# Conditioning products of a two-layer decoder step: six chunk products made three pairs in column halves of TensorE, four chunk buffers, gate spreads between product groups

## The reference

```python
for l in range(DEPTH):
    mod = jax.nn.silu(c) @ w_ada[l] + b_ada[l]          # c: (1 or 8, 1024), w_ada[l]: (1024, 3072)
    shift, scale, gate = jnp.split(mod[:, None, :], 3, axis=-1)
    h = rms_norm(x, g_pre[l]) * (1.0 + scale) + shift
    y, ... = mixer_ab(h, ...) if l == 0 else mixer_c(h, ...)
    x = x + gate * rms_norm(y, g_post[l])
```

## Time and profile before

| what | us |
|---|---|
| median of 3 runs | 2801.58 |
| lowest, highest run | 2794.62, 2807.85 |
| the profiled execution, its own time | 2795.68 |
| its span, first to last instruction | 2793.6 |
| PE busy in it | 2570.5 |
| the conditioning products (line 231), layer 0 | 11.09 to 68.05 |
| the first group of the input product starts | 77.47 |
| the conditioning products, layer 1 | 1005.32 to 1078.36 |

### The profile page before, as it was taken

How to read it: one execution, slowest core, us unless ns; L and a number is a source line. 1 busy time by engine, 2 the same in 40 slices (tenths; PEclk the granted TensorE clock), 3 DMA queues, 4 the chain that set the end, 5 groups by cost and what they waited for, 6 DMA issues and landing times. The chain is left out here.

```text
span 2793.6 us, 53877 instructions
## 1 busy us (share of the span) xinstructions
PE 2570.5 (92%) x20904; PEld 1518.9 (54%) x20968; DVE 1331.8 (48%) x2933; ACT 931.6 (33%) x2672; POOL 773.7 (28%) x849
## 2 busy tenths in 40 slices
PE   7989999999699997997999999985899999999997
PEld 2434444444456642443444444445787888888883
DVE  3230303020478854791653625523566666666535
ACT  2432323133111113442231322234454554545421
POOL 1341101001111111552000000005546465655431
PEclk9899999999899998998999999997999999999977
DMA  8341111122364544653121111115423131313112
GB/s 274 111 147 49 65 64 69 49 72 79 127 211 150 180 137 131 169 153 88 55 74 42 68 58 42 57 49 166 130 66 97 63 100 59 104 55 108 40 39 76
DMA packets 257067, 270.50 MB, mean 97 GB/s; under 512 B 31937, under 2 KB 191057, under 8 KB 256820
## 3 DMA queue, kind: packets, MB, share of 16 engines
q1 hardware_dynamic: 185318, 217.40, 23.9%
q10 hardware_dynamic: 71520, 49.96, 6.5%
HBM read 179.96 MB, written 87.36 MB: 96 GB/s over the span
## 5 line engine op out<-in xcount | busy, mean ns | idle before, releaser
L553 PE MATMUL inc_b<-raw_next,inc_w_hi 128*128 128x512 bf16 (+1 forms) x1522 | 459.0, 383 | 11.7 <-DVE raw_next L470 8.4
L553 PE MATMUL inab_b<-inab_wt,inab_h 128*128 128x512 f16 (+1 forms) x1632 | 360.6, 384 | 13.0 <-POOL inab_wt L506 13.0
L553 PE MATMUL inc_b<-raw_next,inc_w_lo 128*128 128x512 bf16 x734 | 281.0, 383 | 0.0
L553 PEld LDWEIGHTS inab_b<-inab_wt,inab_h 128*128 128x128 bf16 (+3 forms) x1632 | 162.1, 100 | 209.5 <-issue 24.4
L553 PEld LDWEIGHTS inc_b<-raw_next,inc_w_hi 128*128 128x128 f16 x1536 | 151.1, 99 | 190.1 <-DVE raw_next L470 7.6
L462 POOL TENSOR_TENSOR keep<-keep 128x1024 f16<-128x1024 f32 (+1 forms) x26 | 58.3, 2243 | 561.8 <-ACT keep L457 561.8
L553 PE MATMUL inab_b<-inab_h,inab_wc_hi 128*128 128x512 f16 (+4 forms) x712 | 178.9, 346 | 10.6 <-DVE inab_h L470 8.0
L553 PE MATMUL inc_b<-inc_w_hi,raw_next 128*128 128x512 f16 (+2 forms) x784 | 167.1, 311 | 16.9 <-POOL inc_w_lo L506 16.9
L1037 PE MATMUL mixab_y<-keep,mixab_oT_hi 128*128 128x512 f16 (+1 forms) x544 | 163.7, 383 | 5.4 <-DVE mixab_f_y L1063 5.4
L1935 DVE SCALAR_TENSOR_TENSOR inc_acc<-inc_ub,inc_taps,inc_acc 128x512 f32<-128x512 f32 x192 | 152.1, 792 | 6.8
L1842 ACT ACTIVATE inc_ub<-inc_b 128x512 f32<-128x512 f32 x96 | 57.0, 594 | 264.8 <-PE inc_b L553 260.6
(11 more groups left out here) (434 smaller groups left out, 5326.0 us busy)
## 6 DMA issues: line engine op xcount, KB each, us to landing
tmp_qkv<-inc_so SPq DMA_DIRECT2D x96, 256.0 KB, 2.0
mixc_qkv<-tmp_qkv SPq DMA_DIRECT2D x15, 1536.0 KB, 7.7
inc_stage<-in_w_in_c ACTq DMA_DIRECT2D x32, 512.0 KB, 4.5
inab_wt<-in_w_ada SPq DMA_DIRECT2D x6, 2048.0 KB, 9.9
inab_stage<-in_w_in_ab ACTq DMA_DIRECT2D x24, 512.0 KB, 4.1
mixab_cw<-in_w_ada ACTq DMA_DIRECT2D x6, 2048.0 KB, 8.2
keep<-in_x_prompt SPq DMA_DIRECT2D x16, 512.0 KB, 4.7
tmp_v<-inab_vz SPq DMA_DIRECT2D x32, 256.0 KB, 3.8
```

Source lines behind the costliest of these rows:

```text
L553: last = nc.tensor.matmul(dst, lhs(a, k), rhs(b, k), start=(k == 0 and i == 0), stop=(k == KT - 1 and i == len(PASSES) - 1))
```

## The change

It computes the same. Two chunks, 2j and 2j + 1, form a pair: their matmuls alternate k by k, the even chunk's nine rows go to partitions 0 to 8 of one bank, the odd one's to partitions 64 to 72, and so to two column halves of the array. `mod`, `gpre` and `gpost` are kept in the same two row ranges, `load_small` issues six transfers in place of three, and `cond.turn` waits once between its halves.

In layer 0 there are four chunk buffers (the fourth in the room of the low-half channel weights, so POOL's first weight units wait until pair 1 is done), chunk 3 is loaded before tile 2, the tables after chunk 5, and weight unit 0 is loaded after `first_square(2)` and rounded inside the loop. PE's order is turn 0, pair 0, turns 1 and 2, half of pair 1, turn 3, the other half, `cond.turn`, pair 2. The first group waits for h k by k and no longer for the gates; the gates are spread after groups 1 and 3. In layer 1 there are three buffers, the small loads come at the end of the prompt, pairs take the place of the chunks in halves, and DVE's adds come in another order.

```diff
+    def rows(self, n):
+        return slice(n % 2 * HB, n % 2 * HB + C9)
+
+    def part(self, n):
+        return self.mod[self.rows(n), n // 2 * 512:(n // 2 + 1) * 512]
...
+        for e in range(2):
+            bias = self.io["b_ada"][l:l + 1, :].rearrange("o (j e n) -> o j e n", j=3, e=2)[:, :, e, :]
+            eng.dma_start(self.mod[self.rows(e)].rearrange("c (j n) -> c j n", j=3), bias.to_broadcast([C9, 3, 512])).then_inc(self.small_in, 16)
+            for dst, src in ((self.gpre, "g_pre"), (self.gpost, "g_post")):
+                eng.dma_start(dst[self.rows(e)], self.io[src][l:l + 1, e * 512:(e + 1) * 512].to_broadcast([C9, 512])).then_inc(self.small_in, 16)
...
+    def pair(self, pe, j, ks=range(KT)):
+
+        for n in (2 * j, 2 * j + 1):
+            pe.wait_ge(self.w_in[n % self.ring], 16 * (n // self.ring + 1))
...
-        for k in range(KT):
-            last = self.nc.tensor.matmul(self.psM[n][0:C9, :], self.cT[:, k, :], self.w[n % self.ring][:, k, :],
...
+        for k in ks:
+            for n in (2 * j, 2 * j + 1):
+                last = self.nc.tensor.matmul(self.psM[j][self.rows(n), :], self.cT[:, k, :], self.w[n % self.ring][:, k, :],
+                                             start=(k == 0), stop=(k == KT - 1))
+        if KT - 1 in ks:
+            last.then_inc(self.mm, 2)
...
+        for e in range(2):
+            if e:
+                pe.wait_ge(self.even_turned, 1)
+            r = self.rows(e)
+            for n in (e, e + 2):
+                for i in range(4):
+                    k = 4 * n + i
+                    last = self.nc.tensor.transpose(self.psT[:, k * C9:(k + 1) * C9], self.part(n)[:, i * P:(i + 1) * P], self.ident[r, r])
+            last.then_inc(self.modtr if e else self.even_turned, 1)
...
+            before = [i for i in range(j) if self.psG[i] is self.psG[j]]
+            if before:
+                pe.wait_ge(self.gate_ready, before[-1] + 1)
+            sel, n = (self.sel, P) if j < 2 else (self.sel_s, NS)
+            self.nc.tensor.matmul(self.psG[j][0:n, :], sel[self.rows(j), :], self.part(4 + j % 2), start=True, stop=True).then_inc(self.spread, 1)
...
-    cond = Cond(nc, ph, 0, io, modT, ring, w_room[0:C9, 12288:12288 + 3 * D], w_room[0:C9, 15360:15360 + D], r_flat[0:C9, 0:D],
+    ring = [a.rearrange("p (k n) -> p k n", k=KT) for a in (
+        *(w_room[:, i * 4096:(i + 1) * 4096] for i in range(3)),
+        w_chan[1][:].rearrange("p k n -> p (k n)").bitcast(F32)[:, 0:4096])]
...
+    GATES = {1: (0, 1), 3: (2, 3)}
...
+        cond.load(sp, 3)
+        for t in range(2):
+            sp.wait_ge(prep.xnd, t + 1)
+            prep.load(sp, t + 2, t, P)
+        cond.load(sp, 4)
+        cond.load(sp, 5)
...
-        for t in range(TPB):
-            if 3 + t < Cond.CH:
-                cond.load(sp, 3 + t)
-            sp.wait_ge(prep.xnd, t + 1)
-            prep.load(sp, t + 2, t % 2, P)
+        for t in range(2):
+            sp.wait_ge(prep.xnd, t + 3)
+            prep.load(sp, t + 4, t, P)
...
+        sp.wait_ge(ctr, 1)
         sp.wait_ge(cT_ready, 1)
         sp.dma_start(io["cT"], cT[:].rearrange("p k c -> p (k c)")).then_inc(cond.out, 16)
+        sp.sem_inc(u_free, 1)
+        for n in range(4):
+            sp.sem_inc(vz_out[n], 16)
         cond.store(sp)
         sp.wait_ge(cond.out, 48)
-        sp.sem_inc(u_free, 1)
         sp.sem_inc(r_free, 1)
-        for n in range(4):
-            sp.sem_inc(vz_out[n], 16)
...
+        pool.wait_ge(cond.mm, 4)
         for u in (0, 1):
...
+            if t == 0:
+                weights.load(act, 0)
             if t == 1:
-                weights.load(act, 0)
-        weights.hi(act, 0)
+                weights.hi(act, 0)
         weights.hi(act, 1)
         cond.take(act)
+        act.wait_ge(cond.modT_ready, 1)
+        act.sem_inc(evac, RING)
         prep.first_low(act, cond.modT_ready, m_a, m_v, first_hi)
         weights.hi(act, 2)
-        cond.gates(act)
         weights.hi(act, 3)
         act.wait_ge(small_in, 32)
-        act.wait_ge(cond.gate_ready, 4)
-        act.sem_inc(evac, RING)
...
-        dve.wait_ge(cond.small_in, 48)
-        for t in range(TPB):
+        dve.wait_ge(cond.small_in, 96)
+        prep.norm(dve, 0, 0, P)
+        prep.raw_high(dve, 0)
+        prep.norm(dve, 1, 1, P)
+        cond.add(dve, 0)
+        cond.add(dve, 1)
+        prep.raw_high(dve, 1)
+        for t in (2, 3):
             prep.norm(dve, t, t % 2, P)
             prep.raw_high(dve, t)
-            cond.add(dve, t)
+        cond.add(dve, 2)
+        cond.add(dve, 3)
+        prep.first_high(dve, cond.modT_ready, m_v, first_hi, first_lo_p, first_lo_v)
+        for n in (4, 5):
+            cond.add(dve, n)
...
-        for t in range(TPB):
-            cond.chunk(pe, t)
-            prep.turn(pe, t, P)
+        prep.turn(pe, 0, P)
+        cond.pair(pe, 0)
+        prep.turn(pe, 1, P)
+        prep.turn(pe, 2, P)
+        cond.pair(pe, 1, range(KT // 2))
+        prep.turn(pe, 3, P)
+        cond.pair(pe, 1, range(KT // 2, KT))
         cond.turn(pe)
-        for n in (4, 5):
-            cond.chunk(pe, n)
-        cond.spread_gates(pe)
+        cond.pair(pe, 2)
...
+        def first_ready(k):
+
+            pe.wait_ge(first_hi, k + 1)
+            pe.wait_ge(first_lo_v if k % 2 else first_lo_p, k // 2 + 1)
+
+        def groups(b, n, next_tiles, first=False):
+            if not first:
+                pe.wait_ge(prep.h_ready, b + 1)
...
+                if first and g in GATES:
+                    cond.spread_gates(pe, GATES[g])
...
-    ring = [ph.sb(f"cw{i}", [P, KT, 512]) for i in range(2)]
+    ring = [ph.sb(f"cw{i}", [P, KT, 512]) for i in range(3)]
...
+    mod = ph.sb("mod", [P, 3 * 512])
+    gpre, gpost = (a[:].rearrange("p g d -> p (g d)") for a in (S1, U))
...
-        cond.load_small(sp)
...
+        sp.wait_ge(state_ready, nt)
+        cond.load_small(sp)
         store(nt - 1, 1, (nt - 1) // 2, P, 0)
 
-        sp.wait_ge(state_ready, nt)
...
-        for n in range(2):
+        for n in range(3):
             cond.load(act, n)
         with act.Fori(3, nt) as t:
             tile(t)
         fin.square(act, nt - 2, P, 1)
         oT_copy(nt - 1, P)
-        cond.load(act, 2)
...
-        dve.wait_ge(cond.small_in, 48)
-        cond.add(dve, 0)
...
+        dve.wait_ge(cond.small_in, 96)
+        cond.add(dve, 0)
         cond.add(dve, 1)
         by_sequence(0)
         dve.wait_ge(o_done, nt + 1)
         src = lambda h: head(obank, h)[0:NS]
         stats(nt, NS, src)
         norm_gate(nt, 0, NS, src)
+        oT_rest(nt, NS)
+        by_sequence(1)
         cond.add(dve, 2)
-        oT_rest(nt, NS)
         cond.add(dve, 3)
-        by_sequence(1)
...
-                cond.add(dve, 4 + p)
+            if p == 1:
+                cond.add(dve, 4)
+                cond.add(dve, 5)
...
-        cond.chunk(pe, 0)
+        cond.pair(pe, 0, range(KT // 2))
...
-        cond.chunk(pe, 1)
+        cond.pair(pe, 0, range(KT // 2, KT))
...
-        cond.chunk(pe, 2)
+        cond.pair(pe, 1, range(KT // 2))
...
-        cond.chunk(pe, 3)
+        cond.pair(pe, 1, range(KT // 2, KT))
...
-                cond.chunk(pe, 4 + p)
+                cond.pair(pe, 2, range(4 * p, 4 * p + 4))
```

More of the change, by code:

```diff
@@ L546, with product @@
 PASSES = ((0, 0), (0, 1), (1, 0))
-def product(nc, dst, lhs, rhs):
+def product(nc, dst, lhs, rhs, before=lambda k: None):
     for k in range(KT):
+        before(k)
         for i, (a, b) in enumerate(PASSES):
@@ L837, in groups @@
                     weights.hi(act, unit_at[g])
+                if first and g in GATES:
+                    cond.gates(act, GATES[g])
                 if g in rows_at:
@@ L971, in groups @@
                     at = chan_at(c0)
-                    last = product(nc, dst[0:m, 0:n], lambda e, k: w_chan[e][:, k, at:at + m], lambda e, k: prep.h[e][:, k, 0:n])
+                    last = product(nc, dst[0:m, 0:n], lambda e, k: w_chan[e][:, k, at:at + m], lambda e, k: prep.h[e][:, k, 0:n],
+                                   first_ready if first and g == 0 else lambda k: None)
                 elif g < 7:
@@ L989, in groups @@
                         prep.turn(pe, t, r_)
+                if first and g in GATES:
+                    cond.spread_gates(pe, GATES[g])
         for b in range(nb - 1):
-            groups(b, BLK, [(4 * b + 4 + tc, P) for tc in range(4)])
+            groups(b, BLK, [(4 * b + 4 + tc, P) for tc in range(4)], b == 0)
         groups(nb - 1, BLK, [(nt, NS)])
```

57 lines of the change are left out of this document (19 added, 38 removed).

## The result

The changed kernel takes 2780.95 us in the median of five runs (2778.34 to 2786.17), the kernel before 2802.03 in five beside them (2794.62 to 2807.85). By the medians that is 21.1 us or 0.75% less, where 17.5 were forecast. The ratio is 0.9929, with a 95% interval of 0.9909 to 0.995: some 20 us. Two later sets of runs gave 0.9925 (0.9896 to 0.9954) and 0.9939 (0.9917 to 0.996), so 17 to 21 us. The profiled execution took 2784.15 us, its span 2782.4.

What follows compares the result with a forecast made beforehand. PE was taken as the bound, busy 2570.5 of 2793.6 us; layer 0's 11.5 and layer 1's 6 gave 17.5 us off the profiled 2795.7, so 2778.2 (2784.1 against the median), range 2768 to 2803.

Steps and rivals of the forecast that it cites:

- rival C: Both layers' pairs: the halves overlap only partly, 1.6x, 1.8 us more for a pair; 2789 us in all; chance 0.07.
- Step 2: Layer 0: pair 0 starts at 24.3, done at 33.6. Layer 1: the mask at 1026.7 rules, 4.0 us gained.
- Step 4, the new wait: Layer 0: ACT stands at weight unit 0 until 45.2, holding `raw_low(2)` and so PE's turn 3 until 46.1.
- Rival A: Layer 0: weight unit 0 lands in 4 us instead of 9.9 and doesn't hold ACT; 2777 us in all; chance 0.24.
- Steps 5 to 7: Layer 0: half of pair 1 ends at 52.6; four DVE adds, 2.8 us, until 55.4; pair 2 ends at 64.6, first group starts.
- Step 9: Layer 0: gate spreads, now between groups of the input product, cost PE 3.4 us; weight units stay hidden.
- Rival D: Block 0: PE's wait for weight units on POOL grows, layer 0 keeps only 5 us; 2790 us in all; chance 0.13.
- Step 1: Layer 1: half of pair 0 ends early, so the projection starts when `oT_lo` is ready, 1010.6 instead of 1012.29; 1.7 us gained.
- step 3: Layer 1: `turn_o` moves from 1048.42 to 1044.4, still 4.0 us gained; chunk 3 lands at 1033.7, before it is wanted at 1035.9.
- Step 4: Layer 1: pair 1's second half ends at 1050.5, freeing chunk 5's buffer and ACT; `early.turn(0)` goes from 1057.82 to 1052.2, 5.6 us.
- Step 5: Layer 1: pair 2 needs chunks 4 and 5; 5 lands at 1058.7, half the pair done at 1062.5, tile 1 turned 5.6 earlier.
- Rival E: Both layers: the clock stays at 0.50 behind PE's new gaps, costing 25 us; 2809 us in all, slower; chance 0.06.

Runs made afterwards that it cites:

- PE kept at work: Changed kernel plus 18 unread identity products on PE ahead of turn 3 and 18 ahead of `cond.turn` in layer 0; ratio 0.9943 to the kernel before.
- the last combination: Changed kernel with unit 0 later, `cond.take` ahead of unit 1, layer 1's pair 1 whole, 12 identity products ahead of layer 0's `cond.turn`; 2774.84 us, ratio 0.9887.

## Why the prediction came out as it did

The sign, the size and most of the steps held; the time was 3 us below the forecast, within its range. Step by step, for the first and second trace of the changed kernel:

- **Pairs.** Two records for each 0.43 us, as the narrow products of the earlier trace rows had said: 7.04 for a pair where the clock is full, as at 58.51 with PE kept at work and at 51.26 in the last combination. The bound of no overlap and rival C (1.6x) fell. The Trainium skill, "TensorE: Matmul & The Clock Gate", section "Measured speedup vs the span model", would have given 8.7 for a pair; the trace has 7.04, so for two halves of nine columns the measurement decides for 2x.
- **Step 2.** Pair 0 at 25.00 and 24.4, done at 33.75 and 32.8; forecast 24.3 and 33.6.
- **Step 4, the new wait.** Unit 0 landed 9.8 us after its issue in the first trace, as forecast (9.9), and 11.1 in the second. It was issued some 1.5 us earlier than said, so it was rounded at 43.83 and 44.53 (45.2), and turn 3 came at 44.72 and 45.42 (46.1). Rival A (the unit lands in time) had the largest chance of the rivals and fell.
- **Steps 5 to 7.** `cond.turn` at 55.81 and 52.96 (55.4), first group at 67.11 and 62.84 (64.6). The term of the low clock was mis-sized in both directions: 2 us for half of pair 1 and 1 for pair 2, where the first trace shows 1.7 and 2.5, and the second 0 and 1.7, with 1.7 in the first half of pair 1, for which none was counted. Step 6 was mis-sized too: four operations of 0.7, 2.8 in all, are right for the second trace, but in the first they take 4.7, with DVE's scaling of 2.57 beside POOL. That `cond.turn` came within 0.4 us of the forecast there is luck: pair 1 ended 1.6 earlier than said, and the adds took 1.9 longer. The low clock comes after gaps, but behind which of them it falls changes from run to run.
- **Step 8.** Group 0 took 5.5 us: 1.6 gained, 2.0 forecast. **Step 9.** The spreads take 2.2, not 3.4: two go in 1.13 us, four records.
- **Layer 0's sum** was 11.5. By the table it is 16.6 less some 3 in B, 13. Of the 1.5 us short, 1.2 are the spreads; the rest is within the scatter of A, 68 to 72.6. The sum had not seen how much of it hung on the gates' place (some 10 us): it stood in the same 12.9 as the pairs.
- **Rival D.** POOL's waits are 13.0 in three, as before: refuted.
- **Layer 1.** Step 1 was 1.7 (1.67 measured: 5.30 from D's start instead of 6.97), step 2 4.0 (21.47 against 25.44), step 3 4.0 (39.1 against 43.1). Chunk 3's landing was wrong: 28.4 us from D's start and 2.2 before it is wanted by the forecast, 32.4 in the trace. It was issued together with chunk 4, and PE waited 1.67 for it; that hid behind the longer wait ahead of `turn_o`. Step 4 was to be 5.6 and is 4.5: the half pair behind the gap took 6.13 instead of 5.4, and ACT's norm comes after the issue. Step 5: PE waits 3.14 for chunk 5, as said, and turn 1 gains 3.1, not 5.5, since the half pair behind that wait again had a low clock, 5.97 instead of 3.61. Pair 2's last half at full clock, 3.61 instead of a chunk's 7.03, brings `cond.turn` to 6.5 earlier (69.33 against 75.87), and the end gains 7.0 (6 forecast).
- **Rival E, the clock.** Its mechanism is there: a half pair or pair behind a gap costs 1.7 to 2.9 us more. The sum had allowed for that in four places, not behind the wait for chunk 5. In the changed kernel's first 85 us it never lasted beyond the pair behind the gap, where the rival needed it in group 0 and the spreads too.

What the prediction didn't have is the spread between executions: the low clock or its absence behind the same gaps of PE in each block, 3.3 us a block. The execution that it read has the shortest B of all in the table, 627.5. From that one it forecast 2778.2, against 2784.15 in the first trace after; taken from the median, the same difference held.

## What to carry to other kernels

A product of few columns goes twice as fast in two column halves if the records of the halves are issued in turn, but the time follows only as far as PE itself ends the stretch last. In layer 0 the turns of issue gave some 7 us. In layer 1 they gave none beyond what four overlapping records at the seam already give. Look at what stands in the queue between such a product and the next long one, for its place can be worth as much as the speed-up. When two traces of kernels differ in a stretch that the change didn't touch, take a second trace of each before explaining it, and look at the clock behind the gaps that both have.

## What was unexpected of the hardware

- Records that use different halves of the array start together even where the program doesn't alternate: at the seam of two chunks the last four of one ran beside the first four of the other, so that 16 records took 5.33 us instead of 7.04. The odd chunk's first record starts at 43.47, ahead of three of the even chunk's that were issued before it. In that kernel the first group, 16 columns wide, began at 72.41, ahead of the last three records of pair 2 (72.83 to 73.69).
- The two spreads of a pair read rows 0 to 8 and 64 to 72 and write all 128 columns of two banks; their four records of 512 take 1.13 us, where one after the other at 0.43 each would take 1.7 and a tail. So they overlap too.
- The same program has a mean granted clock of 0.97 or 0.98 over 630 us of an unchanged stretch, and 7.7 us of time with it. The low clock follows gaps of 2.1 and 2.5 us in some executions and not in others, and the gaps are the same.
- A DVE operation on 9 x 512 elements took 2.57 us instead of 0.68 in each of the three traces in which a POOL operation of 2.12 us had begun some 0.1 us before it. In the first of them the two ended at 55.76 and 55.21.
